# One plain tile instead of two ahead of the second FFN's seven-product units, and another order of VectorE's weight sums

## The chip, the cores and the metric

One core of a Trainium2 chip runs the whole program. TensorE does the matmuls, VectorE (DVE), ScalarE (ACT) and GpSimd (POOL) the element work, SyncE (SP) issues the weight loads. The metric is device microseconds for one execution; the time of a kernel is the median of its runs. The kernel before: 1295.68 us, median of 3 runs (1295.6 to 1296.47).

## The reference, cut to what matters

One layer over 576 tokens (512 of a prompt and 8 x 8 of decode), width 1024, all float32:

```python
h = x + 0.5 * swiglu(rms_norm(x, g_ffn1), w_ffn1_gu, w_ffn1_down)     # D_FF = 2816 = 22 tiles of 128
u = rms_norm(h, g_mix);  q, k, v, zg, r, us5 = split(u @ w_in)
h = h + concat(GLA(q, k, v, zg, r), S5(us5)) @ w_out                  # S5 needs small matrices made of its parameters
h = h + cross_attend(rms_norm(h, g_cross), memory K/V)
h = h + 0.5 * swiglu(rms_norm(h, g_ffn2), w_ffn2_gu, w_ffn2_down)
y = rms_norm(h, g_final)
# swiglu(x): g, u = split(x @ w_gu);  (silu(g) * u) @ w_down
```

The two FFNs are most of the work. The change is in them, and in where VectorE makes the S5 matrices.

## The kernel before, in words

Every engine has its own list of instructions, written out by hand and run in order; semaphores tie them together. All tokens lie as columns (two halves of 288), features as partitions. A float32 product is done as three passes over high and low parts: high x high, high x low, low x high. ACT rounds a weight block to its high part (`conv` at L1453, into wh) and DVE subtracts it from the raw block for the low part (`conv` at L1967, into wl). `raw` has four slots, filled by SP in block order (`load`, L405).

**Plain blocks.** `dense` is one block of 128 output features: 8 k-tiles x 3 passes x 2 halves = 48 matmuls of 288 columns. An FFN tile of 128 hidden features needs two blocks (gate and up): 96 matmuls. DVE `hidden` multiplies the gate sums with R (the rms factor; L2144), ACT takes silu (L1563), DVE multiplies the up sums with R (L2148) and with the silu (L2151), ACT rounds (`yh`, L1566) and DVE `plain_low` subtracts (`yl`, L2164).

**Seven-product units.** The other FFN tiles are done by a Strassen-Winograd scheme: `unit(v)` on PE makes the gate and up blocks of one tile in seven products of 12 matmuls (84 in place of 96), in the order A11, S1, A12, S2, S4, A22, S3. S1 to S4 are sums of weight quarters, which DVE makes from raw (`sum_of`): S1 (L2055) reads two SBUF blocks and writes PSUM bank 4; S2 (L2058) adds a raw block to bank 4, into bank 5; S4 (L2065) adds one to bank 5, into bank 6; S3 (L2062) reads two SBUF blocks and writes SBUF (`sum3`, one buffer). ACT rounds S1, S2 and S4 in one instruction (`high_sums`, L1502), DVE makes their low parts (`low_sums`, L2071). S3 goes by `high_last` (L1512, and L1514 for A22) and `low_last` (L2076: sum3 minus its high part, two SBUF inputs). POOL makes the low parts of A11 and A12 (L663, 128x1024) and of A22 (L666, 128x512), each behind ACT's rounding (L1494, L1514). The scheme also needs sums of tokens (`token_sums`, `tokens_high`, `tokens_low` at L2085), of which those of k-tile 7 come last.

In `unit(v)` DVE prepares unit v+1 and finishes unit v-1. Its order: S1 of v+1, low_last of v, S2, S3, S4 of v+1, `finish(v-1)` (L2105, L2107, L2109), low_sums of v+1 (L2071), the low part of the hidden tile (L2116), the gate sums of v (L2137, L2139). ACT: high_last(v) (L1512, L1514), keep 1 (L1533, a PSUM sum copied to SBUF), high_gate(v+1) (L1494), keep 2 (L1533), which waits for L2105 of finish(v-1), high_sums(v+1) (L1502), keep 4, the rounding of the hidden tile (L1557), keep 6, silu (L1552). PE starts product S4 of unit v when keep 2 of v is done, product S1 of v when low_sums of v is done, S3 when keep 4 and low_last are done.

**The order of the stages.** FFN1: 4 plain tiles, 4 units, their down blocks; 8 units and down blocks; a third group of 6 plain tiles (12 dense blocks) and down blocks. FFN2: 2 plain tiles (n0 to n0+3), 6 units, down blocks; 8 units, down blocks; 6 units, down blocks. So there are 32 units. `PLAIN` holds how many tiles of a group are plain. Ahead of a group's first unit its sums are made while the last down blocks run.

**S5 matrices.** `matrix_step(o)` on DVE, 24 steps (L2219, L2221, L2223), makes them, steps 0 to 17 beside the third group (one beside a gate block, two beside an up block), the last six beside its down blocks. POOL runs the S5 tables in the same stretch.

**Into FFN2.** `rms(3)` on PE sums the mean squares into banks 4 and 5 while block n0 runs; ACT takes Ln and Exp from there (L1486, L1487); DVE polishes R by three steps (`newton`, L2009 to L2011) that also read the bank. Until then bank 4 can't take a weight sum.

Of the kernel before, what the change touches and what calls it, by code (L numbers as in the profile page):

```python
# [51 lines left out]
def hymba_kernel(nc, A, O, consts):  # L52

    with ExitStack() as ctx:
# [163 lines left out]
        ROWS = dict(prompt=(1, 2, 4, 5), decode=(3, 6))  # L218
        EXPS = dict(prompt=(4, 8, 13, 17), decode=(9, 18))
        TURNS = dict(prompt=(1, 2, 3, 5), decode=(4, 6))  # L220
        HK, PLAIN = KD // 2, {(1, 0): 4, (2, 0): 2, (1, 2): FGROUPS[2]}
        xg = view(MM, 7168, HK, T)
        tok_h, tok_l = view(ARr, 0, HK, 4, TH), view(ARr, 8 * T, HK, 4, TH)
        tok_hf, tok_f = tok_h.bitcast(F32), view(AR, 8 * T, HK, 4, TH)
# [494 lines left out]
        def _(e):  # L719
# [694 lines left out]

            n0 = groups[FFN2]["n0"]
            dense(n0, 0, KD, xh, xl, ready=(x_lo, 24), inside=(lambda: rms(3), KD - 3))
            for b in range(1, 4):
                dense(n0 + b, b % 2, KD, xh, xl)
            seven_group(2)
            seven_group(3)  # L1420
            seven_group(4, each=turn_last)
# [21 lines left out]
        def _(e):  # L1443
# [38 lines left out]
                                 scale=gains[:, G_FINAL, bass.ds(k, 1)]).then_inc(S("yy_ok"), 1)  # L1482

            def rms(m):
                e.wait_ge(ss, m + 1)
                mark(e.activation(R[:], bank(4, T), ACT.Ln, bias=eps[:]), "act_own")  # L1486
                e.activation(R[:], R[:], ACT.Exp, scale=-0.5).then_inc(rt, 1)  # L1487

            def high_gate(v):
# [6 lines left out]

            def high_sums(v):

                e.wait_ge(S("sum_ok"), 4 * v + 4)
                if v >= 2:  # L1500
                    e.wait_ge(S("pr_done"), 7 * v - 9)
                e.activation(operands(v, S1, 3, 0), sums124, ACT.Copy).then_inc(S("hi_ok"), 1)  # L1502

            def high_last(v):

                n = units[v] + 1
                e.wait_ge(S("sum_ok"), 4 * v + 3)
                if v:
                    e.wait_ge(S("pr_done"), 7 * v)
                if v in (0, FIRST_FFN2):  # L1510
                    e.wait_ge(mm_done, seq(n) + 2)
                e.activation(operand(v, S3, 0), sum3, ACT.Copy).then_inc(S("hi_ok"), 1)  # L1512
                e.wait_ge(raw_in[n % 4], 16 * (n // 4 + 1))
                e.activation(operand(v, A22, 0), raw[:, n % 4, 512:1024].rearrange("p (k n) -> p k n", k=HK),  # L1514
                             ACT.Copy).then_inc(S("hi_ok"), 1)
# [398 lines left out]
                    gained(k, G_FFN2)  # L1914

            n0 = groups[FFN2]["n0"]
            for b in range(4):
                i = b // 2
                if b == 0:
                    rms(3)  # L1920
                    tokens_high(KD - 1, base=4 * HK)
                conv(n0 + b + 2)
                if b == 2:
                    high_gate(FIRST_FFN2)
                elif b == 3:
                    high_sums(FIRST_FFN2)
                hidden(i, n0 + b, b % 2, groups[FFN2])
            e.wait_ge(S("t_lo"), 2 * HK)
            e.wait_ge(acc_ready, 24)
            for i in range(2, 5):  # L1930
# [19 lines left out]
        def _(e):  # L1950
# [62 lines left out]
            def rms(m):  # L2013
                if m == 0:
                    e.wait_ge(S("xsq_ok"), NT)
                    own(TSC(row_means, mst[:, 0:NT], 1.0 / D, None, ALU.mult))
                    e.wait_ge(rt, 1)
                    inverse(roots, row_means, row_tmp, "dve_own")
                    for j in range(NT):
                        w = min(P, T - j * P)  # L2020
                        TSC(xdiag[0:w, j * P:j * P + w], ident[0:w, 0:w], roots[0:w, j:j + 1], float(D), ALU.mult, ALU.mult).then_inc(S("xdiag_ok"), 1)
                    e.wait_ge(ss, 1)
                    mark(CP(R[:], bank(4, T)), "r_ready")
                    return
                e.wait_ge(rt, m + 1)
                newton(R[:], bank(4, T), gs[:], "r_ready")

            def down(g):
                def body(i, n, par):
# [88 lines left out]
            def unit(v):  # L2118

                nxt, going = after(v), v not in FIRST_UNIT  # L2120
                if nxt:
                    sum_of(S1, nxt)
                low_last(v)
                if nxt:
                    for j in (S2, S3, S4):
                        sum_of(j, nxt)
                else:
                    conv(units[v] + 2)
                if going:
                    finish(v - 1)  # L2130
                low_sums(nxt) if nxt else conv(units[v] + 3)
                if going:
                    hidden_low(v - 1)
                e.wait_ge(S("pr_done"), 7 * v + 5)
                e.wait_ge(S("e_ok"), 4 * v + 3)
                e.wait_ge(g_act, before(v))
                TTT(two(gs[:]), two(sq[:, 0, :]), halves(1), ALU.add).then_inc(S("c_ok"), 1)  # L2137
                e.wait_ge(S("c_ok"), 2 * v + 1)
                TTT(gs[:], gs[:], R[:], ALU.mult).then_inc(g_scaled, 1)  # L2139
# [26 lines left out]
            def seven_group(i, within=None):  # L2166

                for v in range(FIRST_UNIT[i], FIRST_UNIT[i + 1]):
                    unit(v)
                finish(v)  # L2170
                hidden_low(v)
                g = groups[groups.index(seven_groups[i]) + 1]
                for b in range(KD):
                    n = g["n0"] + b
                    e.wait_ge(mm_done, seq(n) + 3)
                    STT(two(h[:, b, :]), halves(2 * (b % 2)), 0.5, two(h[:, b, :]), ALU.mult, ALU.add).then_inc(ps_free, 1)  # L2176
                    if n == len(blocks) - 1:
                        e.wait_ge(ps_free, seq(n) + 3)
                        TSC(yy[:, b, :], h[:, b, :], gains[:, G_FINAL, b:b + 1], None, ALU.mult).then_inc(S("yy_v"), 1)
                    if b < KD - 2 or i in (1, 4):  # L2180
                        conv(n + 2)
                    if i in (0, 2, 3):
                        if b == KD - 3:
                            for j in (S1, S2, S3, S4):
                                sum_of(j, v + 1)
                        elif b == KD - 2:
                            low_sums(v + 1)
                    if i == 1 and b == 2:
                        second_half_low()
                    if within and b == 4:  # L2190
                        within()

            def parameters_turned():

# [31 lines left out]
            def third_group(i, n, par):  # L2226

                plain_low(i, n, par, groups[4])
                matrix_step(3 * i + par)
                if par:  # L2230
                    matrix_step(3 * i + 2)

            def third_down(i, n, par):

# [35 lines left out]
            conv(2)  # L2270
            rms(0)
            for n in range(8):
                e.wait_ge(mm_done, seq(n) + 3)
                hidden(n // 2, n, n % 2, groups[0])
                if n != 1:
                    conv(n + 3 if n == 0 else n + 2)
                if n == 0:
                    for k in range(HK):
                        token_sums(k)
                elif n == 1:  # L2280
                    for k in range(HK):
                        tokens_low(k)
                elif n < 6:
                    tokens_low(n + 2)
                elif n == 7:
                    low_sums(0)
                plain_low(n // 2, n, n % 2, groups[0])
                if 0 < n < 5:
                    token_sums(n + 3)
                if n == 3:  # L2290
                    parameters_turned()
                elif n == 6:
                    for j in (S1, S2, S3, S4):
                        sum_of(j, 0)
            seven_group(0)
            seven_group(1, within=s5_turned)
# [374 lines left out]
            for k in range(KD):  # L2671
                n = n0 + k
                e.wait_ge(mm_done, seq(n) + 3)
                STT(two(h[:, k, :]), halves(2 * (k % 2)), 1.0, two(h[:, k, :]), ALU.mult, ALU.add).then_inc(ps_free, 1)
                conv(n + 2)
                if k:
                    tokens_low(k - 1, base=KD)
                e.wait_ge(ps_free, seq(n) + 3)
                norm_in(3, k // 2, k % 2)
                token_sums(k, G_FFN2)  # L2680

            n0 = groups[FFN2]["n0"]
            for b in range(4):
                n, i, g = n0 + b, b // 2, groups[FFN2]
                if b == 0:
                    rms(3)
                    conv(n + 2)
                    tokens_low(KD - 1, base=KD)
                e.wait_ge(mm_done, seq(n) + 3)
                hidden(i, n, b % 2, g)  # L2690
                if b:
                    conv(n + 2)
                if b == 3:
                    low_sums(FIRST_FFN2)
                plain_low(i, n, b % 2, g)
                if b == 2:
                    for j in (S1, S2, S3, S4):
                        sum_of(j, FIRST_FFN2)
            for i in range(2, 5):
                seven_group(i)  # L2700
            e.wait_ge(rt, 5)
# [53 lines left out]
```

## Time and profile before

| | |
|---|---|
| median of 3 runs | 1295.68 us |
| the profiled execution | 1296.79 us, its span 1295.0 us |
| PE busy | 1270.0 us, 98% |
| DVE busy | 861.3 us, 67% |
| ACT, POOL busy | 527.3 us, 350.0 us |
| mean granted clock | 0.997 |
| FFN1's second group of units, 160 to 250 us | PE 90.00 of 90.00 us, DVE 77.62, POOL 28.89 |
| FFN2's first group of units, 913.9 to 981 us | PE 64.67 of 67.10 us, DVE 59.96, POOL 22.26 |

How to read it: a timeline row has the start and the duration of an instruction; if it was issued behind the one ahead of it on its engine and had to wait for something other than a semaphore (a port), the wait is in its duration. An idle time in square brackets is a wait for a semaphore and names who released it. "<-PE" or "<-ACT" is the engine that ended the wait.

### The profile page before, as it was taken

The page shows a single profiled execution, that of the slowest core. Times are in us where ns is not written, and L with a number is a line of the kernel's source. Part 1 is how long each engine was busy: PE and PEld are TensorE (multiplying, and loading weights), DVE is VectorE, ACT ScalarE, POOL GpSimd, SP SyncE. Part 2 cuts the span into 40 slices and gives each one's busy share as a digit, 9 for nine tenths or more (in the row PEclk, how much of TensorE's full clock was granted, in tenths as well). Part 3 has the DMA queues.
Part 4 walks back from the last instruction along what each step waited for, and adds up shares of the span by engine and source line. Part 5 has one row for each costly group of instructions (what it writes and reads, how often), then busy time and mean ns, then how long its engine had stood idle before and what let it go on. Part 6 is the DMA issues. An engine that isn't in the chain of part 4 may idle for free.

```text
span 1295.0 us, 24300 instructions
## 1 busy us (share of the span) xinstructions
PE 1270.0 (98%) x10275; PEld 1230.6 (95%) x10275; DVE 861.3 (67%) x1056; ACT 527.3 (41%) x797; POOL 350.0 (27%) x409
## 2 busy tenths in 40 slices
PE   7999999999999999999999999999999999999997
PEld 6999999999999999999999997599999999999997
DVE  4987379844789736558565537478895589637952
ACT  6544145521223422565443224246453255414543
POOL 0025623276896202000002100032230133102321
PEclk9999999999999999999999999999999999999998
DMA  6232233263213442125423656322233323223221
GB/s 185 81 89 82 82 98 98 82 131 88 83 55 85 90 91 63 53 66 153 120 83 97 203 204 225 133 82 79 84 96 85 98 82 99 83 83 96 86 62 73
DMA packets 227148, 129.95 MB, mean 100 GB/s; under 512 B 22240, under 2 KB 221392, under 8 KB 227024
## 3 DMA queue, kind: packets, MB, share of 16 engines
q1 hardware_dynamic: 223168, 123.37, 33.4%
q10 hardware_dynamic: 3872, 5.04, 1.1%
q8 instruction: 81, 1.33, 0.4%
q14 instruction: 27, 0.22, 0.1%
HBM read 121.42 MB, written 5.78 MB: 98 GB/s over the span
## 4 chain that ended last, share of the span: by engine, by line
PE 89%; DVE 6%; ACT 2%; issue 2%; DMA 0%; SPq 0%; DVEq 0%; ACTq 0%
PE PS L723 86%; PE PS L1315 1%; DVE wl L1967 1%; DVE xl L2076 1%; DMA AR<-in_x_prompt 0%; PE PS L791 0%; ACT wh L1453 0%; DVE PS L2055 0%; ACT gua L1599 0%; DVE PS L2221 0%; DVE Hs L2376 0%; PE PS L1401 0%; DVE gua L2151 0%; PE PS L1293 0%; PE PS L933 0%
## 5 line engine op out<-in xcount | busy, mean ns | idle before, releaser
L1453 ACT ACTIVATE wh<-raw 128x1024 fp32r<-128x1024 f32 (+1 forms) x128 | 132.2, 1033 | 377.0 <-PE PS L723 376.9
L723 PE MATMUL PS<-yh,wh 128*128 128x288 f32 x960 | 206.1, 296 | 2.5 <-DVE yl L2164 1.6
L723 PE MATMUL PS<-yl,wh 128*128 128x288 f32 x960 | 205.0, 295 | 0.0
L723 PE MATMUL PS<-yh,wl 128*128 128x288 f32 x960 | 205.0, 295 | 0.0
L1967 DVE TENSOR_TENSOR wl<-raw,wh 128x1024 fp32r<-128x1024 f32 (+1 forms) x128 | 160.1, 1251 | 62.6 <-ACT wh L1453 61.3
L723 PE MATMUL PS<-xh,wh 128*128 128x288 f32 x768 | 171.7, 305 | 0.3 <-DVEq L2146 0.2
L723 PE MATMUL PS<-xh,ARr 128*128 128x288 f32 x768 | 169.5, 296 | 0.3
L723 PE MATMUL PS<-xh,wl 128*128 128x288 f32 x768 | 164.9, 297 | 0.0
L723 PE MATMUL PS<-xl,wh 128*128 128x288 f32 x768 | 164.8, 296 | 0.0
L723 PEld LDWEIGHTS PS<-yh,wh 128*128 128x128 f32 x960 | 154.0, 188 | 4.2 <-DVE yl L2164 1.8
L723 PEld LDWEIGHTS PS<-yh,wl 128*128 128x128 f32 x960 | 154.3, 188 | 0.0
L723 PEld LDWEIGHTS PS<-yl,wh 128*128 128x128 f32 x960 | 154.3, 188 | 0.0
L663 POOL TENSOR_TENSOR ARr<-raw,ARr 128x1024 fp32r<-128x1024 f32 x32 | 81.8, 2556 | 194.8 <-ACT ARr L1494 194.8
L723 PEld LDWEIGHTS PS<-xh,ARr 128*128 128x128 f32 x768 | 128.5, 188 | 0.7 <-ACT sq L1533 0.7
L723 PEld LDWEIGHTS PS<-xh,wh 128*128 128x128 f32 x768 | 123.2, 190 | 3.0 <-issue 1.5
L506 POOL TENSOR_TENSOR acc<-acc,sq 128x576 f32<-128x576 f32 x31 | 52.3, 1687 | 268.4 <-issue 164.4
L723 PEld LDWEIGHTS PS<-xh,wl 128*128 128x128 f32 x768 | 124.1, 189 | 0.0
L723 PEld LDWEIGHTS PS<-xl,wh 128*128 128x128 f32 x768 | 124.0, 189 | 0.0
L723 PE MATMUL PS<-ARr 128*128 128x288 f32 x768 | 111.8, 294 | 3.4 <-DVE ARr L2071 3.4
L723 PE MATMUL PS<-xl,ARr 128*128 128x288 f32 x384 | 113.5, 295 | 0.0
L2176 DVE SCALAR_TENSOR_TENSOR h<-PS,h 128x576 f32<-128x576 f32 x40 | 30.3, 757 | 121.4 <-PE PS L723 121.4
L723 PEld LDWEIGHTS PS<-ARr 128*128 128x128 f32 x768 | 104.8, 188 | 3.9 <-DVE ARr L2071 3.9
(370 smaller groups left out, 2217.0 us busy)
## 6 DMA issues: line engine op xcount, KB each, us to landing
raw<-in_w_ffn_gu SPq DMA_DIRECT2D x88, 512.0 KB, 3.9
raw<-in_w_ffn_down SPq DMA_DIRECT2D x32, 512.0 KB, 4.0
raw<-in_w_in SPq DMA_DIRECT2D x16, 512.0 KB, 4.1
raw<-in_w_ckv SPq DMA_DIRECT2D x16, 512.0 KB, 3.9
raw<-in_w_ffn_down SPq DMA_DIRECT2D x16, 384.0 KB, 3.4
Hs<-in_cache_mem_k SPq DMA_DIRECT2D x6, 1024.0 KB, 7.0
raw<-in_w_out SPq DMA_DIRECT2D x8, 512.0 KB, 4.0
raw<-in_w_cq SPq DMA_DIRECT2D x8, 512.0 KB, 5.1
```

Of the source, the lines that this page charges most:

```text
L506: e.tensor_tensor(acc[:, 0:T], acc[:, 0:T], sq[:, k % 2, :], ALU.add).then_inc(acc_ready, 1)
L663: TTT(operands(v, A11, 2, 1), raw[:, n % 4, :].rearrange("p (s x) -> p s x", s=2), operands(v, A11, 2, 0).bitcast(F32), ALU.subtract).then ...
L723: return e.matmul(out, lhsT, rhs, start=start, stop=stop, **kw)
L1315: last = e.transpose(bank(4 + q % 3, P, at=f * M + j * P), KB[b][:, j, at:at + P], ident)
L1453: e.activation(wh[:, n % 2, 0:K * P], raw[:, n % 4, 0:K * P], ACT.Copy).then_inc(w_hi, 1)
L1967: TTT(wl[:, n % 2, 0:K * P], raw[:, n % 4, 0:K * P], wh[:, n % 2, 0:K * P].bitcast(F32), ALU.subtract).then_inc(w_lo, 1)
L2076: TTT(operand(v, S3, 1), sum3, operand(v, S3, 0).bitcast(F32), ALU.subtract).then_inc(S("lo_s"), 1)
L2176: STT(two(h[:, b, :]), halves(2 * (b % 2)), 0.5, two(h[:, b, :]), ALU.mult, ALU.add).then_inc(ps_free, 1)
```

## The change

1. `PLAIN` for FFN2's first group is 1 and not 2: PE runs n0 and n0+1 as plain blocks, and what were n0+2 and n0+3 become a seventh unit of that group (33 units in all).
2. Ahead of it DVE copies the mean squares from the bank to `us` (SBUF) in the last step of the block before; ACT's Ln and DVE's newton read the copy. Then DVE makes the four weight sums of the first FFN2 unit ahead of newton, and the low sums between the two `hidden` of n0 and n0+1.
3. In every unit S2 and S4 of the next unit go ahead of low_last, S3 stays behind it. The count of `sum_ok` changes accordingly: high_sums waits for three sums, high_last for the fourth.
4. In FFN1 the low sums of the first unit go ahead of the last plain `hidden`.
5. Six of the S5 matrix steps move from the third group to the down blocks of FFN1's second group, so that the third group has one step beside each block.

```diff
-        HK, PLAIN = KD // 2, {(1, 0): 4, (2, 0): 2, (1, 2): FGROUPS[2]}
+        HK, PLAIN = KD // 2, {(1, 0): 4, (2, 0): 1, (1, 2): FGROUPS[2]}
@@ PE
-            for b in range(1, 4):
-                dense(n0 + b, b % 2, KD, xh, xl)
+            dense(n0 + 1, 1, KD, xh, xl)
@@ ACT
             def rms(m):
-                e.wait_ge(ss, m + 1)
-                mark(e.activation(R[:], bank(4, T), ACT.Ln, bias=eps[:]), "act_own")
+                if m == 3:
+                    e.wait_ge(S("mean_ok"), 1)
+                else:
+                    e.wait_ge(ss, m + 1)
+                mark(e.activation(R[:], us[:] if m == 3 else bank(4, T), ACT.Ln, bias=eps[:]), "act_own")
...
-                e.wait_ge(S("sum_ok"), 4 * v + 4)      # high_sums
+                e.wait_ge(S("sum_ok"), 4 * v + 3)
...
-                e.wait_ge(S("sum_ok"), 4 * v + 3)      # high_last
+                e.wait_ge(S("sum_ok"), 4 * v + 4)
...
+            high_gate(FIRST_FFN2)
+            rms(3)
+            tokens_high(KD - 1, base=4 * HK)
+            high_sums(FIRST_FFN2)
+            for b in range(2):
+                hidden(0, n0 + b, b, groups[FFN2])
@@ DVE
+                if m == 3:
+                    for j in (S1, S2, S4, S3):
+                        sum_of(j, FIRST_FFN2)
                 e.wait_ge(rt, m + 1)
-                newton(R[:], bank(4, T), gs[:], "r_ready")
+                newton(R[:], us[:] if m == 3 else bank(4, T), gs[:], "r_ready")
...
                 nxt, going = after(v), v not in FIRST_UNIT      # unit(v)
                 if nxt:
-                    sum_of(S1, nxt)
+                    for j in (S1, S2, S4):
+                        sum_of(j, nxt)
                 low_last(v)
                 if nxt:
-                    for j in (S2, S3, S4):
-                        sum_of(j, nxt)
+                    sum_of(S3, nxt)
...
                     if within and b == 4:
                         within()
+                    elif within and b > 4:
+                        matrix_step(2 * b - 10)
+                        matrix_step(2 * b - 9)
...
                 plain_low(i, n, par, groups[4])                 # third_group
-                matrix_step(3 * i + par)
-                if par:
-                    matrix_step(3 * i + 2)
+                matrix_step(6 + 2 * i + par)
...
             for n in range(8):                                  # FFN1's plain blocks
+                if n == 7:
+                    low_sums(0)
                 e.wait_ge(mm_done, seq(n) + 3)
                 hidden(n // 2, n, n % 2, groups[0])
...
-                elif n == 7:
-                    low_sums(0)
...
+                if k == KD - 1:                                 # the block before FFN2
+                    e.wait_ge(ss, 4)
+                    CP(us[:], bank(4, T)).then_inc(S("mean_ok"), 1)
+                    e.wait_ge(S("mean_ok"), 1)
                 token_sums(k, G_FFN2)
...
+            rms(3)                                              # FFN2's plain blocks
+            for b in range(2):
+                e.wait_ge(mm_done, seq(n0 + b) + 3)
+                hidden(0, n0 + b, b, g)
                 if b == 0:
+                    low_sums(FIRST_FFN2)
+            tokens_low(KD - 1, base=KD)
+            plain_low(0, n0 + 1, 1, g)
```

## Rows read from the trace of the kernel before

**Rows 1.** The page: busy time by engine
```profile
PE 1270.0 (98%) x10275; PEld 1230.6 (95%) x10275; DVE 861.3 (67%) x1056; ACT 527.3 (41%) x797; POOL 350.0 (27%) x409
```

**Rows 2.** Waits of PE: for whom, us in total, times, longest
```profile
PE PS L723 <- DVE ARr L2071: 3.4, 2, 1.7
...
PE PS L723 <- DVE yl L2164: 1.6, 1, 1.6
PE PS L723 <- ACT sq L1533: 1.1, 2, 0.6
...
PE PS L723 <- DVE wl L1967: 0.8, 1, 0.8
```

**Rows 3.** DVE timeline, one unit of FFN2: start us, us, what
```profile
951.17 0.69 DVE L2055 TENSOR_TENSOR PS<-raw 128x512 f32<-128x512 f32 x1
952.52 0.69 DVE L2076 TENSOR_TENSOR xl<-AR,xh 128x512 fp32r<-128x512 f32 x1 [0.66 <-ACT xh L1512]
953.13 0.69 DVE L2058 TENSOR_TENSOR PS<-PS,raw 128x512 f32<-128x512 f32 x1
953.74 1.20 DVE L2062 TENSOR_TENSOR AR<-raw 128x512 f32<-128x512 f32 x1
...
955.46 0.74 DVE L2105 TENSOR_TENSOR gua<-sq,PS 128x576 f32<-128x576 f32 x1
956.24 1.59 DVE L2107 TENSOR_TENSOR gua<-gua,R 128x576 f32<-128x576 f32 x1
...
958.53 1.75 DVE L2071 TENSOR_TENSOR ARr<-PS,ARr 128x1536 fp32r<-128x1536 f32 x1
...
962.33 0.69 DVE L2055 TENSOR_TENSOR PS<-raw 128x512 f32<-128x512 f32 x1
```

**Rows 4.** ACT timeline of the same unit
```profile
953.21 1.05 ACT L1494 ACTIVATE ARr<-raw 128x1024 fp32r<-128x1024 f32 x1
956.24 0.41 ACT L1533 ACTIVATE sq<-PS 128x288 f32<-128x288 f32 x1 [1.98 <-DVE gua L2105]
956.54 1.45 ACT L1502 ACTIVATE ARr<-PS 128x1536 fp32r<-128x1536 f32 x1
```

**Rows 5.** POOL timeline of the same unit
```profile
953.10 1.30 POOL L666 TENSOR_TENSOR xl<-raw,xh 128x512 fp32r<-128x512 f32 x1 [7.05 <-ACT xh L1514]
954.36 2.85 POOL L663 TENSOR_TENSOR ARr<-raw,ARr 128x1024 fp32r<-128x1024 f32 x1
```

**Rows 6.** Windows: a unit; n0+2 and n0+3. Length, PE, PEld, DVE, ACT, POOL busy
```profile
945.61:956.77 11.16, 11.16 (x86) 11.16 (x85) 10.40 (x13) 6.13 (x11) 4.11 (x3) 1.00 0.31 91
...
901.04:913.90 12.86, 12.86 (x97) 12.86 (x98) 6.58 (x9) 5.11 (x6) 2.41 (x1) 1.00 0.35 100
```

**Rows 7.** DVE and POOL timelines, first unit of FFN2
```profile
917.78 1.79 DVE L2055 TENSOR_TENSOR PS<-raw 128x512 f32<-128x512 f32 x1
919.48 2.89 DVE L2076 TENSOR_TENSOR xl<-AR,xh 128x512 fp32r<-128x512 f32 x1
...
917.36 1.65 POOL L666 TENSOR_TENSOR xl<-raw,xh 128x512 fp32r<-128x512 f32 x1 [10.80 <-ACT xh L1514]
918.98 2.86 POOL L663 TENSOR_TENSOR ARr<-raw,ARr 128x1024 fp32r<-128x1024 f32 x1
```

**Rows 8.** DVE timeline, S1 and S2 one right behind the other
```profile
908.58 0.70 DVE L2055 TENSOR_TENSOR PS<-raw 128x512 f32<-128x512 f32 x1 [0.24 <-DVE gua L2144]
909.31 0.70 DVE L2058 TENSOR_TENSOR PS<-PS,raw 128x512 f32<-128x512 f32 x1
```

**Rows 9.** ACT and PE timelines, FFN2's second group, third unit: keep 2, product S4
```profile
1060.83 0.41 ACT L1533 ACTIVATE sq<-PS 128x288 f32<-128x288 f32 x1 [1.53 <-DVE gua L2105]
...
1062.44 0.30 PE L723 MATMUL PS<-xh,ARr 128*128 128x288 f32 x1
```

**Rows 10.** DVE timeline, a matrix step at the end of FFN1's third group
```profile
394.65 2.45 DVE L2221 TENSOR_TENSOR PS<-AR 128x1152 f32<-128x1152 f32 x1
```

**Rows 11.** DVE timeline, last step of newton at the head of FFN2
```profile
897.05 0.76 DVE L2011 SCALAR_TENSOR_TENSOR R<-gua,R 128x576 f32<-128x576 f32 x1
```

More of the change, by code:

```diff
@@ L1916, in _ @@
             n0 = groups[FFN2]["n0"]
[L1917 to L1927, printed above, removed]
+            high_gate(FIRST_FFN2)
[4 more added lines that the diff above has]
+                hidden(0, n0 + b, b, groups[FFN2])
             e.wait_ge(S("t_lo"), 2 * HK)
@@ L2183, in seven_group @@
                         if b == KD - 3:
-                            for j in (S1, S2, S3, S4):
+                            for j in (S1, S2, S4, S3):
                                 sum_of(j, v + 1)
@@ L2292, in _ @@
                 elif n == 6:
-                    for j in (S1, S2, S3, S4):
+                    for j in (S1, S2, S4, S3):
                         sum_of(j, 0)
@@ L2679, in _ @@
                 norm_in(3, k // 2, k % 2)
+                if k == KD - 1:
+                    e.wait_ge(ss, 4)
+                    CP(us[:], bank(4, T)).then_inc(S("mean_ok"), 1)
+                    e.wait_ge(S("mean_ok"), 1)
                 token_sums(k, G_FFN2)
             n0 = groups[FFN2]["n0"]
-            for b in range(4):
-                n, i, g = n0 + b, b // 2, groups[FFN2]
-                if b == 0:
[L2686 to L2693, printed above, removed]
+            g = groups[FFN2]
+            rms(3)
+            for b in range(2):
+                e.wait_ge(mm_done, seq(n0 + b) + 3)
+                hidden(0, n0 + b, b, g)
+                if b == 0:
                     low_sums(FIRST_FFN2)
[L2695 to L2698, printed above, removed]
+            tokens_low(KD - 1, base=KD)
+            plain_low(0, n0 + 1, 1, g)
             for i in range(2, 5):
```

## The prediction

> **What bounds the kernel now.** I read the busy times first: PE works 1270.0 of 1295.0 us [rows 1], so less PE work or less waiting of PE is all that can be won, and at most 25 us of the second kind. The list of PE's waits says where [rows 2]: 3.4 us in two waits for the low sums (L2071), 1.1 us in two for ACT's keep 4 (L1533), 1.6 and 0.8 us at the third group of FFN1 for DVE's yl and wl. The first two kinds are one wait at the first unit of each FFN's first group, so 1.7 + 0.55 us a place; with a third of about 0.3 us, which the start times show in the unit behind it, 2.6 us a place.
>
> Then the timelines inside a unit, since 32 units make 32 x 11.16 = 357 us of the time. A unit's 84 matmuls take 11.16 us [rows 6], and DVE's own round, from S1 (L2055) to the next S1, takes 962.33 - 951.17 = 11.16 us too [rows 3]. DVE waits for nothing in it but 0.66 us for ACT's L1512. The page's 67% for DVE is an average: in the units of a large group PE has no slack against DVE, and each microsecond that DVE's round grows is one that PE waits, in every unit.
>
> What fills DVE's round are also two waits without a bracket, inside durations. L2062 (S3) takes 1.20 us while L2055, with the same shape, takes 0.69; L2107 takes 1.59 us while L2105 takes 0.74 [rows 3]. Both have both inputs in SBUF and both lie in a POOL instruction: L666 runs from 953.10 to about 954.39, and S3 ends at 954.94, 0.55 us behind it; L663 ends at 957.21, and L2107 at 957.83 [rows 3, 5]. L2058 and L2105 have one input in PSUM, start within the same POOL instructions, and take their usual 0.69 and 0.74. So a DVE instruction with two SBUF inputs stands still until the POOL instruction ahead of it ends; one with a PSUM input doesn't.
>
> **The change part by part.**
>
> *The order within a unit (point 3).* This decides the forecast. In the old order the two blocked instructions are far apart, and unblocked ones (S2, S4, L2105) lie behind POOL's two. In the new order S1, S2 and S4 are done early, and low_last and S3, both with two SBUF inputs, stand one behind the other just where POOL starts. In us from S1's start (951.17 is 0):
> - S1 at 0, S2 at 0.73 and S4 at 1.46 (each reads the bank of the one before; 909.31 - 908.58 = 0.73 [rows 8]), low_last at 1.46 + 0.61 = 2.07 (952.52 to 953.13 is such a distance [rows 3]). The 0.66 us of waiting for L1512 are gone.
> - POOL's L666 starts at 953.10, that is 1.93, and hangs on ACT, whose order is as before. It is 0.14 us ahead of low_last, which now waits until 3.2 and ends at 3.75.
> - POOL's L663 is asked for at 3.19 (954.36), behind ACT's L1494 [rows 4, 5]. S3 must wait for low_last (one buffer) and is asked for at 3.8. Which goes first? The first unit of FFN2 shows this very case [rows 7]: L2055 was blocked by L666 until 919.57, L663 had been waiting from 918.98, low_last was issued at 919.48 and didn't end until 922.37, 0.53 us behind the end of L663 (921.84). So POOL's next instruction goes ahead of DVE's next one, and S3 ends at 6.04 + 0.55 = 6.6, not at 3.8.
> - finish's L2105, at 4.29 before [rows 3], starts at 6.6; keep 2, at 5.07 before [rows 4], at 7.35; high_sums 0.30 behind it at 7.65, to 9.10 (1.45); low_sums need high_sums and start at 9.15 instead of 7.36 (958.53). L2107 and L2109 run from 7.35 to 8.85 and don't add. The rest of the round is as before.
>
> So the round grows by 9.15 - 7.36 = 1.8 us, from 11.16 to 12.95. Once DVE is behind PE, POOL's L663 is always ready in time (keep 1 no longer waits for PE ahead of L1494), so the pattern holds itself. PE meets it as a wait of S4 for keep 2.
>
> How many units pay: in a group of eight, unit 0 has no finish and unit 1 still gets L1512 late. In unit 2 keep 2 starts 2.3 us later; it had 1062.44 - 1061.24 = 1.2 us to spare [rows 9], so 1.0 to 1.1 us. Units 3 to 6 pay 1.8 each. The last unit prepares no successor. That is 1.0 + 4 x 1.8 = 8.2 us, in FFN1's second group and FFN2's second. The last group has six: 1.0 + 2 x 1.8 = 4.6. Bounds of the round: from +0.5 (S3 gets in ahead of L663, rival 1) to +2.3 (low_last and S3 each lose the whole of a POOL instruction beyond the old waits); below nothing only if the 0.66 us are all that counts (rival 2). I take 1.8 because rows 7 show the nearest case.
>
> *FFN1's first group (points 3 and 4).* low_sums(0) moves into DVE's idle time ahead of the last hidden; S1 of the first unit no longer waits, and high_sums come earlier, so keep 4 is in time: the 2.6 us go. But PE then is 2.6 us further on, with DVE where it was. PE starts the group at 72.3 and wants unit 1's S4 eleven products of 1.59 us later (11.16 / 7), at 89.8. DVE starts unit 0 at 76.1 (76.3 before), loses POOL's L663 at low_last as before, and reaches S1 of unit 1's round at 84.4 (87.3 before); L2105 comes 6.5 later at 90.9, keep 2 is over at 92.1, and PE has waited 2.4 us. Unit 2 pays 1.8. Sum: 4.2 - 2.6 = +1.6.
>
> *FFN2's head and first group (points 1 to 3).* n0+2 and n0+3 go, 12.86 us, and a unit comes, 11.16 [rows 6]: -1.7 us. On DVE the copy (0.75, like an evacuation of the same bank), the token sums behind it and four weight sums (4 x 0.7) now stand ahead of newton, whose end moves from 897.81 [rows 11] to 900.3. The hidden of n0 ends at 901.05, where PE wants A11 of the first unit at 900.65: 0.5 us (0.2 us are lost there now). S1 wants the low sums (1.75) and the second hidden (0.76) behind that, 903.6, and A11 ends at 902.75: 0.9. With 0.1 at S2 for keep 1, 1.5 us. In exchange the 2.6 and the 0.2 go. Then unit 1 pays 2.6 as in FFN1 and units 2 to 5 pay 1.8 each, 9.8 in all. Sum without the matmuls: 1.5 + 9.8 - 2.8 = +8.5. Cover: the weight loads of n0+2 and n0+3 are issued behind the conversions of n0-2 and n0-1 as before and have landed by then. SP's later loads wait for sum_ok of S3 and for L666 and L663 of a unit; the slots are wanted a whole unit later, so a shift of some 3 us costs nothing.
>
> *The S5 steps (point 5).* The third group's up blocks lose one step each. The last (2.45 us with its waits for POOL, [rows 10]) stood ahead of the conversion for which PE waited 0.8 us [rows 2]: that wait goes. Of the 1.6 us wait for yl, which stands behind two blocked instructions and not behind a step, I take 0.5. So -1.3; the bounds are 0 and -2.4. The six steps fall into the down blocks of FFN1's second group, where DVE is idle 3.7 to 4.0 us a block and a pair of steps takes 2.6: nothing. If they didn't fit, the first block of the third group would be late by what is over, under 1 us.
>
> The Trainium skill (SBUF — State Buffer, section "Who interferes with whom") says that a DVE instruction with two SBUF inputs contends with a GpSimd instruction that reads SBUF, and that the one issued first holds the shared pair for its whole length. By that rule, too, L663 (asked for at 3.19) goes ahead of S3 (3.8), and the sum stays. It names no order for when the pair comes free with both sides wanting it; if it went to DVE, rival 1's sum would hold.
>
> **The sum.** FFN1's first group +1.6, its second +8.2, the third -1.3; FFN2's first +8.5 - 1.7, its second +8.2, its last +4.6: +28.1 us. On the profiled execution, 1296.8 us (span 1295.0 and 1.8 around it), that is 1324.9; the median of the runs is 1.1 us below that execution, so 1324.
>
> **The rivals.**
> 1. S3 slips in ahead of L663. For it: the two requests are only 0.6 us apart, and L663 has just been held back. Against it: rows 7. Then L663 ends at 6.65, L2107 at 7.2 instead of 6.65, and the round grows by 0.5: 15 coupled units x 0.5 = 7.5 us, with the gains below almost cancelled and some 2 us left of the first collisions: about 1299.
> 2. Faster. If low_last and S3 don't collide with POOL (it decides whether L666 starts ahead of low_last, a margin of 0.14 us, and whether PE's pace then keeps L663 behind S3 by way of keep 1), the round gets no longer, and the gains stand alone: 2.6 + 1.3 + 1.7 + (2.8 - 1.6) = 6.8 us, so 1289.
> 3. The new order isn't felt at all, since POOL drifts to another phase in which only some groups collide: half of the +28, 1310. Nothing in the rows speaks for it; ACT drives both POOL instructions from the same point in each round.
>
> **How the numbers follow.** Forecast 0.65, with 1317 to 1332 as its own range (the round's growth 1.3 to 2.3 on 15 units); rival 3 0.08; rival 1 0.10; rival 2 0.17. The forecast and rival 3 are slower by over 0.2% (2.6 us, what a measurement of this kernel can tell from no change), of rival 1 most is slower and the rest the same: slower 0.80, same 0.04, faster 0.16. The range 1298 to 1332 leaves out rival 2.
>
> **What would show it.** L2062 at about 2.8 us in place of 1.20 in the inner units and L2076 at 1.6 in place of 0.69; L2105 12.95 us apart; PE waits for ACT's L1533 summing to over 30 us; the wait for L2071 in FFN1 gone; L2221's wait for wl gone. Wrong if L2062 stays at 1.2 or less, or if L2105 comes every 11.2 us or less.

## The result, and the profile after

The changed kernel takes 1325.32 us (1323.69 to 1327.24, 4 runs) against 1295.74 us: ratio 1.0226, 95% interval 1.0210 to 1.0242, so 29.6 us slower. Forecast were 1324 us and slower.

The page of the changed kernel: busy time by engine, and the chain that ended last by engine.

```profile
PE 1274.8 (96%) x10263; PEld 1232.1 (93%) x10263; DVE 918.1 (69%) x1063; ACT 525.7 (40%) x803; POOL 357.0 (27%) x411
...
PE 72%; DVE 16%; issue 7%; ACT 3%; DMA 0%; SPq 0%; DVEq 0%; ACTq 0%
```

PE has about the same work as in [rows 1], 12 matmuls less. DVE is busy 57 us more with seven instructions more. 47 of them lie in three kinds: S3 (L2062) takes 71.5 us in all instead of 33.3, low_last (L2076) 45.0 instead of 26.5, and L2107 32.8 instead of 42.9. Each runs only once more than before (33 times for 32); what has grown is the waits for the port, which count as busy. The list of PE's waits answers to [rows 2] (columns as there):

```profile
PE PS L723 <- ACT sq L1535: 25.4, 18, 2.4
...
PE PS L723 <- issue: 1.4, 2, 0.7
PE PS L723 <- DVE wl L1964: 1.3, 2, 0.9
PE PS L723 <- DVE yl L2164: 1.3, 1, 1.3
```

The two waits for low sums (3.4 us) and the two for keep 4 are gone. In their place are 18 for keep 2 (L1535 in the new file); the two that stand as "issue" are A11 and S1 of FFN2's first unit. Inside a unit the timeline of DVE, FFN1's second group, answers to [rows 3]:

```profile
218.67 0.69 DVE L2055 TENSOR_TENSOR PS<-raw 128x512 f32<-128x512 f32 x1
219.40 0.70 DVE L2058 TENSOR_TENSOR PS<-PS,raw 128x512 f32<-128x512 f32 x1
220.13 0.70 DVE L2065 TENSOR_TENSOR PS<-PS,raw 128x512 f32<-128x512 f32 x1
220.74 1.70 DVE L2076 TENSOR_TENSOR xl<-AR,xh 128x512 fp32r<-128x512 f32 x1
222.48 2.77 DVE L2062 TENSOR_TENSOR AR<-raw 128x512 f32<-128x512 f32 x1
225.16 0.74 DVE L2105 TENSOR_TENSOR gua<-sq,PS 128x576 f32<-128x576 f32 x1
225.94 0.76 DVE L2107 TENSOR_TENSOR gua<-gua,R 128x576 f32<-128x576 f32 x1
```

And POOL's of the same unit, to [rows 5]:

```profile
220.59 1.30 POOL L666 TENSOR_TENSOR xl<-raw,xh 128x512 fp32r<-128x512 f32 x1 [8.76 <-ACT xh L1516]
221.85 2.84 POOL L663 TENSOR_TENSOR ARr<-raw,ARr 128x1024 fp32r<-128x1024 f32 x1
```

low_last (L2076) was issued at 220.74, 0.15 us behind L666, and ends 0.55 us behind it, at 222.44. L663 had been issued at 221.85, S3 (L2062) only at 222.48: L663 goes first, to 224.69, and S3 ends at 225.25. L2105 starts 6.49 us behind S1, where it was 4.29. L2107, with nothing of POOL beside it now, is back at 0.76 us, but too late. The window of one round of PE, length and busy times, answers to the first of [rows 6]:

```profile
213.55:226.41 12.86, 11.40 (x85) 11.16 (x85) 12.41 (x13) 6.01 (x11) 4.10 (x2) 1.00 0.28 83
```

12.86 us in place of 11.16 for the same 84 matmuls. Of the 1.70 us more PE waits 1.45, which ends with this matmul, and is busy 0.24 longer (11.40 for 11.16):

```profile
213.55 0.40 PE L723 MATMUL PS<-xh,ARr 128*128 128x288 f32 x1 [1.45 <-ACT sq L1535]
```

L2105 follows L2105 by 12.85 or 12.86 us wherever two units in a row have the collision. Unit 2 of each FFN's first group hasn't got it. There PE had been late (last section), ACT's L1514 and keep 1 waited for it, and POOL's two came later (DVE's, then POOL's timeline, FFN1):

```profile
98.46 0.69 DVE L2076 TENSOR_TENSOR xl<-AR,xh 128x512 fp32r<-128x512 f32 x1
99.19 1.69 DVE L2062 TENSOR_TENSOR AR<-raw 128x512 f32<-128x512 f32 x1
...
99.03 1.30 POOL L666 TENSOR_TENSOR xl<-raw,xh 128x512 fp32r<-128x512 f32 x1 [9.61 <-ACT xh L1516]
100.82 2.40 POOL L663 TENSOR_TENSOR ARr<-raw,ARr 128x1024 fp32r<-128x1024 f32 x1 [0.49 <-ACT ARr L1496]
```

low_last got in ahead of L666, S3 was held by L666 alone and went ahead of L663, and L2105 came 4.54 us behind S1 instead of 6.49.

Where the time went, by the start of PE's first matmul of each stage in its timeline (us, in the profiled executions):

| stage | before | changed | difference | forecast |
|---|---|---|---|---|
| FFN1's first group, A11 to its down blocks | 47.74 | 48.14 | +0.4 | +1.6 |
| down blocks and second group | 140.18 | 148.35 | +8.2 | +8.2 |
| from there to FFN2's mean squares | 631.15 | 631.67 | +0.5 | -1.3 |
| FFN2's head and first group | 92.54 | 97.85 | +5.3 | +6.8 |
| down blocks and second group | 138.94 | 148.28 | +9.3 | +8.2 |
| down blocks and last group | 117.93 | 122.57 | +4.6 | +4.6 |

In the fifth row 1.25 us are the pace of matmuls in eight down blocks of that execution of the kernel before (last section); without them it is +8.1. The rows sum to +28.4 us; with what lies ahead of the first and behind the last, the spans of the two profiled executions differ by 26.7 us. The medians differ by 29.6, since the profiled execution was the fastest of the changed kernel and the slowest of the kernel before.

### The profile page after: what moved, and what is told of

Read it like the earlier page. It is cut to its first block, busy times and chain, and to the rows that moved or that the text cites. A ratio compares the mean times of both kernels' runs of the same rounds, so it can differ in the third digit from the quotient of the medians.

```text
span 1321.7 us, 24301 instructions
## 1 busy us (share of the span) xinstructions
PE 1274.8 (96%) x10263; PEld 1232.1 (93%) x10263; DVE 918.1 (69%) x1063; ACT 525.7 (40%) x803; POOL 357.0 (27%) x411
## 4 chain that ended last, share of the span: by engine, by line
PE 72%; DVE 16%; issue 7%; ACT 3%; DMA 0%; SPq 0%; DVEq 0%; ACTq 0%
PE PS L723 68%; DVE xl L2076 3%; DVE ARr L2071 1%; ACT ARr L1504 1%; DVE gua L2105 1%; DVE PS L2058 1%; DVE PS L2055 1%; DVE PS L2065 1%; DVE gua L2137 1%; DVE yl L2116 1%; PE PS L1315 1%; DVE gua L2107 1%; PE PS L791 1%; DVE wl L1964 0%; ACT wh L1452 0%
## 5 line engine op out<-in xcount | busy, mean ns | idle before, releaser
L723 PE MATMUL PS<-xh,ARr 128*128 128x288 f32 x792 | 178.3, 301 | 26.1 <-ACT sq L1535 25.4
L1964 DVE TENSOR_TENSOR wl<-raw,wh 128x1024 fp32r<-128x1024 f32 (+1 forms) x126 | 154.5, 1226 | 62.0 <-ACT wh L1452 60.9
L723 PE MATMUL PS<-xh,wh 128*128 128x288 f32 x736 | 164.8, 305 | 0.1
L723 PEld LDWEIGHTS PS<-xh,ARr 128*128 128x128 f32 x792 | 134.1, 190 | 30.5 <-ACT sq L1535 29.6
L723 PE MATMUL PS<-xh,wl 128*128 128x288 f32 x736 | 158.0, 296 | 0.0
L723 PE MATMUL PS<-xl,wh 128*128 128x288 f32 x736 | 157.9, 296 | 0.0
L663 POOL TENSOR_TENSOR ARr<-raw,ARr 128x1024 fp32r<-128x1024 f32 x33 | 86.8, 2631 | 183.4 <-ACT ARr L1496 183.4
L1535 ACT ACTIVATE sq<-PS 128x288 f32<-128x288 f32 x132 | 53.9, 409 | 176.5 <-PE PS L723 89.2
L723 PEld LDWEIGHTS PS<-xh,wl 128*128 128x128 f32 x736 | 118.9, 189 | 0.0
L723 PEld LDWEIGHTS PS<-xl,wh 128*128 128x128 f32 x736 | 118.8, 189 | 0.0
L666 POOL TENSOR_TENSOR xl<-raw,xh 128x512 fp32r<-128x512 f32 x33 | 43.0, 1303 | 263.9 <-ACT xh L1516 263.9
```

What stands on the lines that cost most here:

```text
L663: TTT(operands(v, A11, 2, 1), raw[:, n % 4, :].rearrange("p (s x) -> p s x", s=2), operands(v, A11, 2, 0).bitcast(F32), ALU.subtract).then ...
L666: TTT(operand(v, A22, 1), raw[:, (n + 1) % 4, 512:1024].rearrange("p (k n) -> p k n", k=HK), operand(v, A22, 0).bitcast(F32), ALU.subtract ...
L723: return e.matmul(out, lhsT, rhs, start=start, stop=stop, **kw)
L1535: e.activation(out, bank(b, TH), ACT.Copy, **kw).then_inc(S("e_ok"), 1)
L1964: TTT(wl[:, n % 2, 0:K * P], raw[:, n % 4, 0:K * P], wh[:, n % 2, 0:K * P].bitcast(F32), ALU.subtract).then_inc(w_lo, 1)
```

## The experiments

Each kernel's ratio is to the kernel before, measured beside it. e1 to e4 ran on one chip and e5, e7, e8 and e9 on another, and the changed kernel was measured apart from both, so differences from it go by the ratios.

The theory: low_last and S3, both with two SBUF inputs, one behind the other at the point where POOL's two instructions run, cost 1.7 to 1.8 us a unit; the rest of the change is worth a few us. Rivals: the loss comes from FFN2's head, the copy or the matrix steps; or from DVE having too much to do in the new order, whatever POOL does.

### e1_old_unit_order: the changed kernel, old order inside the units

The edit in DVE's list; `front(v)` is true for the first unit of a group. ACT's two counts of `sum_ok` (left out) follow it.

```diff
                 if nxt:
-                    for j in (S1, S2, S4):
+                    for j in ((S1, S2, S4) if front(nxt) else (S1,)):
                         sum_of(j, nxt)
                 low_last(v)
                 if nxt:
-                    sum_of(S3, nxt)
+                    for j in ((S3,) if front(nxt) else (S2, S3, S4)):
+                        sum_of(j, nxt)
```

> The changed kernel with the old order inside the units (S1, low_last, S2, S3, S4); only the first unit's prefetched sums keep the new order. Theory (low_last and S3, both with two SBUF inputs, stand one behind the other where POOL's two instructions run): L2062 back to 1.20 us, L2105 11.16 us apart, the 25 us of waits for keep 2 gone. But in each FFN's first unit keep 4 again waits behind high_sums, now by about 2 us, since PE comes there 1.9 us earlier and DVE doesn't: the early low sums give nothing by themselves. Sum against the kernel before: 1.7 us of matmuls less, about 1.3 us more at FFN2's head, 0.4 less in FFN1: about 1295 (1292 to 1298). Rival (the loss lies in the head of FFN2, the moved matrix steps or the copy of the mean squares): it stays above 1310.

Measured: 1291.81 us (1290.75 to 1293.41, 6 runs), ratio to the kernel before 0.9972 (0.9960 to 0.9984). The whole loss goes with the order inside the units. DVE's timeline of an inner unit (S3 is L2066 here, low_last L2080, L2107 is L2111):

```profile
214.43 0.69 DVE L2059 TENSOR_TENSOR PS<-raw 128x512 f32<-128x512 f32 x1
215.78 0.69 DVE L2080 TENSOR_TENSOR xl<-AR,xh 128x512 fp32r<-128x512 f32 x1 [0.66 <-ACT xh L1518]
216.39 0.69 DVE L2062 TENSOR_TENSOR PS<-PS,raw 128x512 f32<-128x512 f32 x1
217.00 1.21 DVE L2066 TENSOR_TENSOR AR<-raw 128x512 f32<-128x512 f32 x1
...
218.73 0.74 DVE L2109 TENSOR_TENSOR gua<-sq,PS 128x576 f32<-128x576 f32 x1
219.50 1.59 DVE L2111 TENSOR_TENSOR gua<-gua,R 128x576 f32<-128x576 f32 x1
```

It was 0.2 us under my bounds. I had keep 4 late by 2 us in both FFNs; PE's waits show 1.2 us in FFN1 and none in FFN2:

```profile
PE PS L727 <- ACT sq L1539: 1.2, 1, 1.2
```

### e2_unit_order_alone: the kernel before, new order of the sums alone

The edit is point 3 of the change and nothing else.

> The kernel before with the new order of the sums alone (point 3, in the units and in the prefetch). Theory: the second group of FFN1 +7.5, FFN2's second +7.5 and last +4.3, FFN2's first group +3 (its first unit still waits 1.8 us for the low sums, so PE arrives later and meets the blocked finish later), FFN1's first group about 0: +22 us, 1318 (1313 to 1322), L2105 12.86 us apart in the inner units. Rival (the loss needs the other points too): under 1305.

Measured: 1321.61 us (1319.9 to 1322.89, 4 runs), ratio 1.0199 (1.0183 to 1.0214). The order alone makes +25.8 us by the ratio, over the +22 expected and at the top of its bounds. PE's waits: 22.5 us for keep 2 and the two waits for low sums still there, as in [rows 2]:

```profile
PE PS L723 <- ACT sq L1533: 22.5, 17, 1.5
...
PE PS L723 <- DVE ARr L2071: 3.4, 2, 1.7
```

### e3_pool_behind_s3: the changed kernel with one more wait on POOL

```diff
                     e.wait_ge(S("hi_ok"), 4 * v + 1)
+                    if v not in FIRST_UNIT:
+                        e.wait_ge(S("sum_ok"), 4 * v + 4)
                     TTT(operands(v, A11, 2, 1), ...)      # L663
```

> The changed kernel, in which POOL also waits for S3 of the coming unit before L663. Nothing is taken away; a wait is added. Theory (who holds the port): S3 then goes right behind low_last, L663 runs from about 4.5 to 6.8 us of the round and blocks L2107 only; the round is 11.85 in place of 12.86 us and L2062 takes about 0.7 us: 1.0 us less on 15 units and some 4 on the first collisions, so about 1306 (1302 to 1311). Rival (DVE has too much to do in the new order whatever POOL does, or S1, S2, S4 in a row are themselves slow): no faster than 1322.

Measured: 1302.54 us (1302.08 to 1304.56, 4 runs), ratio 1.0057 (1.0041 to 1.0074). A wait is added, and the ratio falls from 1.0226 to 1.0057, which is 22 us. DVE's and then POOL's timeline of a unit (two lines further down in this file: S3 is L2064, L663 is L665):

```profile
214.79 1.70 DVE L2078 TENSOR_TENSOR xl<-AR,xh 128x512 fp32r<-128x512 f32 x1
216.53 0.69 DVE L2064 TENSOR_TENSOR AR<-raw 128x512 f32<-128x512 f32 x1
217.14 0.75 DVE L2107 TENSOR_TENSOR gua<-sq,PS 128x576 f32<-128x576 f32 x1
217.92 2.43 DVE L2109 TENSOR_TENSOR gua<-gua,R 128x576 f32<-128x576 f32 x1
```

```profile
214.65 1.30 POOL L668 TENSOR_TENSOR xl<-raw,xh 128x512 fp32r<-128x512 f32 x1 [7.04 <-ACT xh L1518]
217.37 2.37 POOL L665 TENSOR_TENSOR ARr<-raw,ARr 128x1024 fp32r<-128x1024 f32 x1 [1.42 <-DVE AR L2064]
```

S3 is back at 0.69 us in the same DVE order, and the instruction that stands still for POOL is the next one with two SBUF inputs, behind L2107 (the finish), which keep 2 needs. PE's waits for keep 2 fall from 25.4 to 9.1 us. DVE's order is thus not slow by itself; what costs is who holds the port when S3 asks. The time lies in the bounds, but one step of the expectation was off: L2105 follows L2105 by 12.12 to 12.17 us in most units and not by 11.85. It isn't quite rival 1 of the prediction (S3 ahead of L663, 1299): here L663 starts only behind S3, 4.64 us behind S1, and L2107 ends at 7.6 where rival 1 had 7.2.

### e4_new_order_first_units: new order where there is no finish

As e1, with `front(v)` true also for the unit behind a first one, so that the first unit of each group prepares S1, S2, S4 ahead of low_last.

> The changed kernel with the new order only in the first unit of each group (where DVE has no finish to do), the old order in all others. Theory: both gains at once. L2105 11.16 us apart, no wait for keep 4 in the first units: FFN1's first group 2.5 us better than before, FFN2's first 0.9 better and 1.7 less of matmuls, the matrix steps about nothing: 1290.5 (1288 to 1293), faster than both kernels. Rival (the first units' gain is lost again a unit later): same as the first of these kernels, 1295.

Measured: 1291.82 us (1288.96 to 1292.62, 5 runs), ratio 0.9962 (0.9949 to 0.9975). The same kernel once more, e9_first_units_again:

> The fourth kernel once more, beside these on the same chip and in more rounds: 1291 (1289.5 to 1292.5), faster than the kernel before by 0.2 to 0.5%.

1291.55 us (1289.31 to 1292.58, 5 runs), ratio 0.9962 (0.9948 to 0.9976). Faster than both kernels, by 0.4% on the one before. Against e1 the intervals overlap, so that the order in the first units adds something isn't shown by the times. In the traces it adds 1.9 us in FFN1 and nothing in FFN2: FFN1's first group takes 44.50 or 44.51 us in e4, e7, e8 and e9, 46.41 in e1 and 47.74 before, and the wait of 1.2 us for keep 4 is gone; FFN2's head and first group take 89.57 us in e4 and 89.25 in e1.

### e7_without_short_head: e4 without points 1 and 2

> The fourth kernel (new order in first units only) without points 1 and 2: FFN2 again has two plain tiles and newton reads the bank. It keeps the early low sums in FFN1, the new order in the first units and the moved steps. Theory: FFN2 then has the 12.86 us of two blocks and loses the 11.16 of a unit (+1.7), the head's 1.4 us of waits go (-1.4 + 0.2), and the first unit of FFN2 waits 1.7 us for the low sums again; so about 2 us slower than the fourth kernel, 1293.5. Rival (the seventh unit's shorter work is eaten by its head): equal to the fourth kernel.

Measured: 1293.09 us (1292.12 to 1294.2, 11 runs), ratio 0.9977 (0.9968 to 0.9986); 1.5 us more than e9, which is e4 on the same chip, where the theory had 2. In the traces FFN2's head and first group take 91.15 us here and 89.63 in e9. PE waits 1.7 us for the low sums of FFN2 again.

```profile
PE PS L727 <- DVE yl L2169: 1.8, 1, 1.8
PE PS L727 <- DVE ARr L2075: 1.7, 1, 1.7
```

The intervals of the ratios (0.9968 to 0.9986 and 0.9948 to 0.9976) still overlap, so the times alone don't show the 1.5 us.

### e5_steps_alone and e8_without_steps: the S5 matrix steps

e5 is the kernel before with point 5 alone, e8 is e4 without it.

> The kernel before with point 5 alone (six matrix steps ahead of the third group). The prediction gave it -1.3 us. The traces of the changed kernel and of the first of these kernels already speak against it: there PE waits 1.3 us for yl and 0.4 + 0.9 for wl in that stretch, 2.6 in place of 1.6 + 0.8. Theory now: it only moves POOL's and DVE's collisions about, 0 (1294.5 to 1297). Rival (the prediction's term): 1294.4 or less.

> The fourth kernel without point 5 (the matrix steps where they were). If point 5 moves nothing: the same time as the fourth kernel, 1291.8 within 0.6, with PE's waits there back at 1.6 and 0.8. If the collisions it causes cost something: up to 1 us faster than the fourth kernel, and the best version.

Measured: e5 1295.89 us (1295.37 to 1297.71, 11 runs), ratio 1.0005 (0.9996 to 1.0015); e8 1291.77 us (1289.8 to 1293.09, 6 runs), ratio 0.9967 (0.9955 to 0.9978). The times show nothing won: the 1.3 us forecast would be 0.9990, just under e5's interval. PE's waits in e5, then in e8, beside those of [rows 2]:

```profile
PE PS L723 <- DVE wl L1967: 1.3, 2, 0.9
PE PS L723 <- DVE yl L2164: 1.1, 1, 1.1
...
PE PS L727 <- DVE yl L2169: 1.6, 1, 1.6
PE PS L727 <- DVE wl L1968: 1.0, 1, 1.0
```

1.6 + 0.8 became 1.1 + 1.3 in e5, and in e8, without the moved steps, it is 1.6 + 1.0. The traces show a little more than the times: from the first matmul of the third group's down blocks to PE's first matmul behind them are 41.30 or 41.31 us in the three kernels with the steps where they were (before, e2, e8), 41.58 to 41.61 in e3, e4, e5 and e9, 41.77 in the changed kernel, 41.78 in e1 and 41.97 in e7 (there with a stretch at half clock, last section). So point 5 costs 0.3 to 0.5 us there; that is also most of the +0.5 in the third row of the table of stages.

## Why the prediction was right, and where it wasn't

- **The unit's round (the step that decided).** Right in place and nearly in size: 12.86 us measured, 12.95 forecast, since L2105 started 6.49 us behind S1 and not 6.6, and all behind it 0.1 us earlier. Who goes first at the port was rightly read from rows 7. The margin on which it hung, L666 0.14 us ahead of low_last, was 0.15, and it isn't safe: in unit 2 of both first groups it was lost and S3 went ahead of L663 by itself, as above. e3 shows what letting S3 in gives. The three groups of 8, 8 and 6 are +8.2, +8.1 and +4.6 against 8.2, 8.2 and 4.6.
- **The signs.** Those on the unit's round came (2.77, 1.70 and 12.86 us), and the wait for L2071 is gone. Two didn't: PE's waits for keep 2 sum to 25.4 us and not to over 30, and the waits for wl grew to 1.3 us. For the first, a unit costs PE 1.45 us of waiting and 0.24 of busy time where I had put all 1.8 into the wait, and unit 2 of the two first groups doesn't wait at all.
- **Luck in the total.** 1325.3 for 1324 is closer than its terms: FFN1's first group is 1.2 us under its forecast and FFN2's 1.5, the S5 steps are 1.8 over, and these nearly cancel. The term that carries the result, 21 of the 28 us, was right without that.
- **The Trainium skill** (SBUF — State Buffer, "Who interferes with whom") has the rule behind it: a DVE instruction with two SBUF inputs contends with a GpSimd instruction that reads SBUF, one with at most one SBUF input doesn't. The traces agree in both halves: S2, S4 and L2105 take 0.69 to 0.74 us beside POOL in the kernel before, while instructions with both inputs in SBUF end 0.5 to 0.6 us behind POOL's. What it leaves open, who is next when both sides wait, the trace bears on: L666 is followed by low_last (issued at 220.74) and not by L663 (221.85), and then L663 goes ahead of S3 (222.48). So neither engine always has precedence; the one that was issued first goes first. A rule by turns would give the same here, and no run tells the two apart.
- **FFN1's first group.** +0.4 for the forecast +1.6: DVE's S1 of the first unit came at 74.89 where my walk had 76.1, of which 0.65 us are the earlier start of the whole stage in this execution. Unit 1 then waited 1.86 us and not 2.4. Unit 2 showed no wait of 1.8: PE had run at half clock in between (last section) and arrived late itself, and with that the collision of this unit didn't come about, as above. The forecast had neither.
- **FFN2's head and first group.** The two small waits are there, 0.7 and 0.7 us where I had 0.5 and 0.9, and newton ended at 908.90, which is 2.65 us later than before measured from the block ahead (2.5 forecast). The seventh unit for two blocks is worth what e7 shows, about 1.5 us. The group came out at +5.3 for +6.8, with unit 2 again without its collision.
- **The S5 steps.** Wrong: -1.3 forecast; nothing in the times and 0.3 to 0.5 us more in the traces (e5, e8). The step that failed is "that wait goes": the 0.8 us for wl became 1.3 in two waits. I took one DVE instruction out of a chain with several that are held by POOL's; the waits only changed places (in the changed kernel the yl of the last block took 1.82 us instead of 1.59, and the conversion ahead of it 1.80 as before). That the chain's length is set by POOL's instructions is my reading; no run changed them.
- **The gains.** Rival 2's sum, the change without the collision, was -6.8 us; e4, the nearest to it, measured -4.9 by its ratio (0.0038 x 1295.9). Without the S5 term the sum is -5.5.

## What to carry to other kernels

Where DVE and POOL both read SBUF, order DVE's list so that instructions with a PSUM input lie beside POOL's, and no two with two SBUF inputs follow each other while two of POOL's are due; here such a pair put the next instruction of DVE 2.2 us later. Where the order has to stay, a wait on POOL can bring most of it back (e3), but not all. Removing a semaphore wait (0.66 us here) from a round that is closed over several engines can move an instruction to a worse place; walk the round with the other engines' start times before believing it. And a wait that is no semaphore wait shows only as a duration that is longer than the same shape's minimum, so compare an instruction's durations with their minimum before reading an engine as busy.

## What the runs showed of the hardware that I had not expected

Behind each of the two long waits for keep 2 in unit 1 (1.9 and 2.4 us, with half of the preceding microseconds idle) the granted clock fell to its lower level, 1.2 GHz, for 3.4 us, while DVE was busy throughout. Windows of the changed kernel: length, PE, PEld, DVE, ACT and POOL busy, granted clock, DMA:

```profile
87.50:91.10 3.60, 1.78 (x14) 1.55 (x12) 3.57 (x3) 0.42 (x2) 1.92 (x1) 1.00 0.51 146
...
91.10:95.20 4.10, 4.06 (x19) 4.06 (x20) 3.83 (x5) 2.20 (x3) 0.00 (x0) 0.58 0.45 132
95.20:99.00 3.80, 3.80 (x31) 3.80 (x31) 3.65 (x6) 2.14 (x4) 0.00 (x0) 1.00 0.00 0
...
931.00:935.00 4.00, 4.00 (x18) 4.00 (x19) 3.73 (x5) 2.15 (x3) 0.00 (x0) 0.57 0.45 133
```

19 matmuls in 4.1 us where the next window has 31 in 3.8. By the two paces 3.4 us at half clock are about 1.7 us of work, an estimate. What it cost the kernel isn't shown: PE's wait in the next unit fell away, but its lateness also moved POOL's instructions in that unit (the lines of unit 2 above). e7 had such a stretch too, behind its wait of 1.8 us for yl:

```profile
392.00:395.00 3.00, 3.00 (x15) 3.00 (x14) 2.44 (x3) 1.88 (x3) 2.83 (x3) 0.50 0.23 66
```

The waits of 1.5 us that follow each other every 12.86 us never did this, nor did the two of 1.7 us in the kernel before. What decides wasn't tried.

The second is a pace: in some down blocks a matmul of 288 columns follows the last after 130 ns, in the others after 133 ns, at the same granted clock. Eight blocks of the kernel before (983.9 to 1033.8 us) took 49.93 us where the same eight take 51.19 in e1 and e4. It came and went between executions (no group in the changed kernel, one in the kernel before, in e5, e8 and e9, two in e3), and accounts for 1.25 us a time. Its cause stays open; it is a reason not to read a microsecond out of one pair of profiles.
